# A two-layer decoder trunk: more buffers behind the attention transposes, bf16 weight copies in DRAM, and input norms computed inside the preceding MLP

## The reference

```python
def pool_mixer(a, w, scale):   # trailing mean over 2/4/8/16 positions, minus the token, then a linear map
def stick_breaking_attention(q, k, v):            # strictly causal, 8 heads of 64, no softmax
    z = einsum(q, k) / 8
    log_keep = where(mask, log_sigmoid(-z), 0)
    suffix = cumsum_from_the_right(log_keep) - log_keep
    weights = where(mask, exp(log_sigmoid(z) + suffix), 0)
    o = einsum(weights.astype(v.dtype), v)
for layer in range(2):
    xn = rmsnorm(h, mix_norm_g[layer])
    ...                                           # the two mixers of the layer, concatenated
    h = h + mixers @ w_out
    h = h + square(relu(rmsnorm(h, mlp_norm_g[layer]) @ w1)) @ w2
return rmsnorm(h, final_norm_g)
```

## Time and profile before

| | us |
|---|---|
| median of 3 runs | 3643.56 (3628.75 to 3654.9) |
| the profiled execution | 3627.29 |
| its span, slowest core (core 0) | 3625.8 (cores: 3571.9 to 3625.8) |
| PE busy | 2988.4 (82%) |
| DVE, ACT, POOL busy | 1440.2, 1375.5, 1126.3 |
| DMA packets | 381.62 MB, of which 189.02 MB on POOL's queue and 189.67 MB on SP's |

### The profile page before, as it was taken

One profiled execution on the slowest core, in us unless ns is written; L12 is line 12 of the kernel. 1 busy time (PEld: TensorE's weight loads), 2 busy tenths in 40 slices (PEclk: granted clock), 3 DMA queues, 4 the chain that ended last, 5 costly groups with the idle time before them and its releaser, 6 DMA issues.

```text
span 3625.8 us, 45548 instructions; the slowest of 8 cores (3571.9 to 3625.8 us)
## 1 busy us (share of the span) xinstructions
PE 2988.4 (82%) x14779; PEld 1287.9 (36%) x15073; DVE 1440.2 (40%) x1829; ACT 1375.5 (38%) x2277; POOL 1126.3 (31%) x1622
## 2 busy tenths in 40 slices
PE   1999867898888888788878688989889867888898
PEld 0444333343333333333333233333333323333343
DVE  2410426432434535763335363325444444434212
ACT  1244332525335353343434335242453435252522
POOL 1411125233123433633331342331244423432110
PEclk9999988999999999999989899999999988999999
DMA  7444684556677665656566555565666576567543
GB/s 180 67 68 79 125 171 72 74 91 96 121 172 97 112 90 97 137 88 88 88 103 132 133 86 73 90 101 107 128 96 99 91 169 85 93 96 153 104 76 82
DMA packets 466070, 381.62 MB, mean 105 GB/s; under 512 B 307760, under 2 KB 324400, under 8 KB 465840
## 3 DMA queue, kind: packets, MB, share of 16 engines
q0 software_dynamic: 103824, 189.02, 35.3%
q1 hardware_dynamic: 362016, 189.67, 24.1%
HBM read 454.30 MB, written 41.94 MB: 137 GB/s over the span
## 4 chain that ended last, share of the span: by engine, by line
PE 48%; DMA 24%; DVE 9%; POOL 6%; issue 5%; ACT 4%; SPq 4%; DVEq 0%; POOLq 0%; ACTq 0%
PE ps L543 44%; DMA Wk<-Wq 17%; DMA stg<-xT 5%; DVE P L1121 4%; POOL Wq L1135 4%; SPq L536 3%; PE ps L1160 2%; ACT ps L533 2%; PE ps L1105 1%; DMA oT<-stg 1%; DVE X_45 L619 1%; DMA mix<-dsp 1%; POOL Wq L1138 1%; DVE st_58 L936 0%; DVE h L650 0%
## 5 line engine op out<-in xcount | busy, mean ns | idle before, releaser
L543 PE MATMUL ps<-X_45,ring 128*128 128x512 bf16 x4746 | 1118.4, 389 | 23.0 <-DVE X_45 L619 6.1
L533 ACT ACTIVATE ps<-ps 128x512 f32<-128x512 f32 (+3 forms) x832 | 577.2, 698 | 836.7 <-PE ps L543 518.0
L569 POOL DMA_DIRECT2D ring<-wblk x720 | 391.4, 547 | 1391.3 <-PE ps L543 1180.6
L543 PE MATMUL ps<-mix,ring 128*128 128x512 bf16 x2980 | 756.0, 400 | 48.4 <-DMA mix<-dsp 28.9
L1135 POOL TENSOR_TENSOR Wq<-P 128x1022 bf16<-128x1022 f32 (+2 forms) x320 | 524.2, 1638 | 609.5 <-DVE P L1121 608.0
L1121 DVE TENSOR_TENSOR_SCAN P<-ps,carry,zeros 128x512 f32<-128x512 f32 x384 | 490.2, 1280 | 496.5 <-ACT ps L533 463.6
L543 PEld LDWEIGHTS ps<-X_45,ring 128*128 128x128 bf16 x4864 | 469.8, 100 | 592.4 <-issue 89.0
L650 DVE TENSOR_TENSOR h<-ps,h 128x512 f32<-128x512 f32 x384 | 263.7, 687 | 865.6 <-PE ps L543 845.1
L543 PE MATMUL ps<-ffB,ring 128*128 128x512 bf16 x2007 | 486.9, 384 | 2.3 <-issue 0.2
L543 PEld LDWEIGHTS ps<-mix,ring 128*128 128x128 bf16 x3072 | 297.2, 102 | 418.5 <-issue 126.2
L1160 PE MATMUL ps<-Wk,V 128*64 128x128 bf16 x2176 | 129.3, 236 | 337.2 <-DMA Wk<-Wq 336.1
(11 more groups left out here) (107 smaller groups left out, 1236.3 us busy)
## 6 DMA issues: line engine op xcount, KB each, us to landing
ring<-wblk POOLq DMA_DIRECT2D x720, 256.0 KB, 5.2
stg<-xT SPq DMA_DIRECT2D x128, 256.0 KB, 5.5
h<-xT SPq DMA_DIRECT2D x64, 256.0 KB, 16.2
hsp<-h SPq DMA_DIRECT2D x64, 256.0 KB, 5.1
h<-hsp SPq DMA_DIRECT2D x64, 256.0 KB, 8.0
oT<-stg SPq DMA_DIRECT2D x64, 256.0 KB, 3.3
Wk<-Wq SPq DMA_TRANSPOSE x320, 3.6
csp<-mix SPq DMA_DIRECT2D x8, 512.0 KB, 5.1
```

Of the source, the lines that this page charges most:

```text
L533: return Req("act", lambda e: e.activation(out=out, in_=in_, func=func, **kw), reads, writes, dur, bias=bias)
L543: ins = pe.matmul(out, lhsT=l, rhs=r, start=(first and i == 0), stop=(last and i == n - 1), skip_group_check=True)
L569: yield Req("pool", (lambda slot, b: lambda e: e.dma_start(out=self.ring[:, slot, :], in_=self.wblk[b]))(slot, b), [], [self.Lring[slot]], ...
```

## The change

Five things are changed.

1. `NWT` goes from 4 to 7 landing buffers, and the planned landing of a transpose from 3.1 to 7.0 us. Room in SBUF comes from `chain_pool`: two ping-pong buffers and a bf16 buffer become one (`PS`), the shifted adds run in place with all operands read from right to left, and the bf16 result overlays the same buffer.
2. A DRAM tensor `wbf` keeps a bf16 copy of every weight block. The first load of a block still casts from `wblk`; then SP stores the slot to `wbf` (`keep_block`), and the slot cannot be reused until that store has read it (`release`). Later loads of the block read `wbf`. First loads fall in F00 (88), M00 (20) and S00 (72).
3. `prefetch_x` for the next F stage is started right after the last input projection of the current one, so its norm matmuls, squares and scalings stand in that stage's output projection and MLP.
4. The first F stage has its own `start_x`: `x` is loaded straight into `h` (16 transfers, once), and squares and scalings read `h`.
5. In S, `load_mix` is started ahead of the reload of `h`.

```diff
-NWT = 4
+NWT = 7
...
     def ring_fiber(self):
         for n, b in enumerate(self.order):
             slot = yield self.slots
+            src = self.wbf if b in self.Lwbf else self.wblk
...
+            if b not in self.Lwbf:
+                self.Lwbf[b] = LT("wbf")
+                self.busy.add(slot)
+                self.M.spawn(self.keep_block(slot, b), 0.5)
             self.loaded[n] = slot
+
+    def keep_block(self, slot, b):
+        yield self.dma(self.wbf[b], self.ring[:, slot, :], [self.Lring[slot]], [self.Lwbf[b]], ("keep", slot))
+        self.busy.discard(slot)
+        if slot in self.gone:
+            self.gone.discard(slot)
+            self.slots.free(slot)
...
+    def start_x(self):
+        X, LX = self.X[0], self.LX[0]
+        for t in range(2):
+            ts = slice(t * TT, (t + 1) * TT)
+            for c in range(8):
+                yield self.load_h(self.xT, None, 0, 0, t, c)
+        for t in range(2):
...
+            for c in range(8):
+                yield self.act(X[:, c, ts], self.h[:, c, ts], AF.Square, [self.Lh[c][t]], [LX[c][t]], TT, False)
+            yield from self.norm(X, LX, t, None, 0, self.to_X(t, 0))
+            self.xready.add((0, 0, t))
...
                 yield Req("pool", (lambda src, d, b0: lambda e: e.tensor_tensor(
+                    out=S1[:, b0:528][:, ::-1], in0=src[:, b0:528][:, ::-1], in1=src[:, b0 - d:528 - d][:, ::-1],
+                    op=ALU.add))(src, d, b0), [Ls], [L1], 1.15)
...
-        self.xfree = True
+        if nx:
+            self.M.spawn(self.prefetch_x(*nx), 1.0)
         yield from self.out_proj("F", s, u)
...
-                  key=("wk", k), lat=3.1)
+                  key=("wk", k), lat=7.0)
...
+        self.M.spawn(self.load_mix(s, u), -0.2)
         self.M.spawn(self.load_h_fiber(self.hsp, self.Lhsp, s, u, self.hfree, "S"), 0.0)
-        self.M.spawn(self.load_mix(s, u), 0.0)
...
-        M.spawn(self.prefetch_x(0, 0), -0.5)
+        M.spawn(self.start_x(), -0.5)
```

More of the change, by code:

```diff
@@ L568, in ring_fiber, with release @@
             slot = yield self.slots
-            yield Req("pool", (lambda slot, b: lambda e: e.dma_start(out=self.ring[:, slot, :], in_=self.wblk[b]))(slot, b),
-                      [], [self.Lring[slot]], 0.53, key=("ring", slot), lat=4.0, bias=1.0)
-            self.loaded[n] = slot
+            src = self.wbf if b in self.Lwbf else self.wblk
+            yield Req("pool", (lambda slot, b, src: lambda e: e.dma_start(out=self.ring[:, slot, :], in_=src[b]))(slot, b, src),
+                      [self.Lwbf[b]] if b in self.Lwbf else [], [self.Lring[slot]], 0.53, key=("ring", slot),
+                      lat=4.0, bias=1.0)
+            if b not in self.Lwbf:
+                self.Lwbf[b] = LT("wbf")
+                self.busy.add(slot)
+                self.M.spawn(self.keep_block(slot, b), 0.5)
+            self.loaded[n] = slot
+    def keep_block(self, slot, b):
[4 more added lines that the diff above has]
+            self.slots.free(slot)
+    def release(self, slot):
+        if slot in self.busy:
+            self.gone.add(slot)
+        else:
+            self.slots.free(slot)
     def take(self, n):
@@ L738, in mlp @@
                         if t == 1:
-                            self.slots.free(sl[j])
+                            self.release(sl[j])
                 self.use_scratch("ff")
@@ L744, in mlp @@
                     yield from w1(sl[0], j, t)
-                self.slots.free(sl[0])
+                self.release(sl[0])
             n = 8 if q == 0 else 4
@@ L750, in mlp @@
                     yield from w2(sl, c, t, q)
-                self.slots.free(sl[0])
-                self.slots.free(sl[1])
+                self.release(sl[0])
+                self.release(sl[1])
             if q == 1:
@@ L758, in mlp @@
                         if t == 1:
-                            self.slots.free(sl[2 * c - 8])
-                            self.slots.free(sl[2 * c - 7])
+                            self.release(sl[2 * c - 8])
+                            self.release(sl[2 * c - 7])
             self.ffgen += 1
@@ L857, in chain_pool, with stage_F @@
         return evac
-    def stage_F(self, s, u):
+    def stage_F(self, s, u, nx):
         X, LX = self.X[0], self.LX[0]
@@ L863, in stage_F @@
         self.use_scratch("l0")
-        self.M.spawn(self.load_h_fiber(self.xT, None, s, u, self.hfree, "F"), 0.5)
+        if (s, u) != (0, 0):
+            self.M.spawn(self.load_h_fiber(self.xT, None, s, u, self.hfree, "F"), 0.5)
         for i in range(4):
@@ L922, in out_proj @@
                 if t == 1:
-                    self.slots.free(sl[c])
+                    self.release(sl[c])
     def chain_v(self, s, u, n, v):
@@ L1008, in stage_M @@
                 for x in sl[0:4]:
-                    self.slots.free(x)
+                    self.release(x)
             for g in range(4):
@@ L1017, in stage_M @@
                 if t == 1:
-                    self.slots.free(sl[4 + g])
+                    self.release(sl[4 + g])
         yield from self.need_attention(2 * s + u)
@@ L1237, in main @@
             if kind == "F":
-                yield from self.stage_F(s, u)
                 nx = [x for x in self.stages[n + 1:] if x[0] == "F"]
-                if nx:
-                    self.M.spawn(self.prefetch_x(nx[0][1], nx[0][2]), 1.0)
+                yield from self.stage_F(s, u, nx[0][1:] if nx else None)
             elif kind == "M":
@@ L1253, in build @@
         self.loaded = {}
+        self.Lwbf = {}
+        self.busy = set()
+        self.gone = set()
         self.blk = 0
```

50 lines of the change are left out of this document (23 added, 27 removed).

## The result

The changed kernel takes 3185.54 us (median of 4 runs, 3177.98 to 3210.77), the kernel before, run beside it, 3636.15 (median of 4, 3619.26 to 3654.9). The ratio is 0.8771, 95% interval 0.8714 to 0.8828: faster by 12.3 per cent. The forecast was 3225 us with a range of 3105 to 3355.

The account below looks back on a forecast made before the run. PE was taken to bound the kernel, losing time to late transposes (336.1 us) and half clock (486 us). 3627.3 - 258 - 80 - 33 - 40 - 14 + 10 + 8 = 3220, stated as 3225 us, range 3105 to 3355.

Parts of the forecast that it names:

- the likeliest case: The prediction's own forecast for the whole kernel, 3130 to 3330 us, given a chance of 0.60.
- waits for transposes: PE's value products waiting for late transposes: 336 us, less 58 beyond 3.7 us and 20 left in S00, -258 us.
- clock, as shorter busy time of PE: Whole core: granted clock rises from 0.933 towards F00's 0.97, worth at most 134 us; 0.6 of it taken, -80 us.
- start, waits up to the second tile's projection: First F stage: first projection at about 48 us, 19 us earlier, and second tile's waits gone; -33 us.
- input norms, waits outside the start: F stages: the 40.4 us of input waits "go", -40 us; 10 us charged for work moved into the stage before.
- `mix`: S stages: loading `mix` before the reload of `h` saves half of 28.9 us of waits, -14 us.
- The reason given for the copies: Weight loads: 540 non-casting loads save 0.9 us of engine time each, so the gain is in shorter transposes.
- 8 us longer for the stores: F00: stores of copies beside casting loads raise DMA share to 0.80, which fits; 8 us charged, ends 0 and 30.
- More: Rival: nearly all transposes land in 3 us, and waits and slow clock vanish; 3040 to 3130 us, chance 0.16.
- Half: Rival: PE arrives earlier but the chains do not; only 168 us of waits and 40 of clock go; 3350 us, 0.17.
- No change: Rival: another engine, nearest ACT in the MLP's first half, binds once PE stops waiting; 3600 to 3660 us, chance 0.04.
- Slower: Rival: POOL's reversed adds, each costing 5.1 us more than 1.04, eat the whole gain; chance 0.03.

Follow-up runs that it names:

- r_after: The changed kernel itself, word for word, timed and profiled a second time; median 3181.1 us, ratio 0.8749 to the kernel before.
- e_cast2: The changed kernel without bf16 copies: all 720 weight loads cast and nothing is stored; 3234.46 us, ratio 0.8888 to the kernel before.
- two-by-two: Four kernels: planned transpose landing 7.0 or 3.1 us (distance 64 or 48 matmuls), each with and without bf16 copies; ratios 0.8749, 0.8888, 0.9297, 0.9582.
- e_lat31_cast: The changed kernel with planned transpose landing back at 3.1 us and no bf16 copies; 3488.9 us, ratio 0.9582 to the kernel before.
- e_lat31: The changed kernel with planned transpose landing back at 3.1 us, copies kept; 3382.7 us, ratio 0.9297 to the kernel before.
- e_nwt4: The changed kernel with 4 landing buffers instead of 7; 3185.62 us, ratio 0.8744 to the kernel before.
- e_oldpre: The changed kernel with the next F stage's input loaded and normed after the F stage, beside the M stage, as before; 3238.69 us, ratio 0.893.
- e_nostart: The changed kernel with the first F stage's input loaded as before, by `prefetch_x`, and `h` loaded again; 3246.35 us, ratio 0.8963.
- b_lat7: The kernel before with only the planned transpose landing changed, 7.0 us instead of 3.1; 3350.7 us, ratio 0.9231.
- i_lat10_stg: The changed kernel with planned landings of 10.0 us for transposes, 5.0 for staged `x` loads, 6.5 for first weight loads; 3144.56 us, ratio 0.865.

## Why the prediction was right, and where its steps were off

The total was 40 us too high, inside the range, and the likeliest case was the one that came. How good its terms were depends on how they are counted, since the parts of the change cover for each other.

**By the rows of the two profiles.** PE's idle time fell from 3625.8 - 2988.4 = 637 to 3179.1 - 2917.2 = 262 us, its busy time by 71. Forecast and measured, by term:

| | forecast | rows of `before` and `r_after` |
|---|---|---|
| waits for transposes | -258 | -281 (336.1 to 54.9) |
| clock, as shorter busy time of PE | -80 | -71 |
| start, waits up to the second tile's projection | -33 | -38 |
| input norms, waits outside the start | -40 + 10 | -15 (40.4 to 25.0) |
| `mix` | -14 | -12 (28.9 to 17.3) |

The trace of the kernel before lacks 294 of PE's 15073 matmuls, so its busy time is rather larger than the row says, by an estimated 13 us (the 12.8 us in 68 idle moments that nothing released, of which `r_after` has none). Some 30 us of the 447 are in rows too small for this table. By this account the large terms, transposes and clock, were right in kind and in size; the terms err both ways, by 2 to 23 us, and that these errors partly cancel is luck. The waits came out at 54.9 us where 78 were forecast, with five over 4 us and S00 the worst of the stretches:

```profile
PE ps L1194 <- DMA Wk<-Wq: 22.4, 10, 6.4
```

(`r_after`, PE's waits in S00 alone: 22.4 of 54.9; in `e_cast2`, without stores, S00 has 8.8 of 80.0.) The clock came to 0.970, the cap of the prediction, and not to the 0.6 of the way there that it took. That the busy time fell by less than the 134 us of that cap fits the prediction's reason, that PE stands still in part of the slow time.

**By the kernels of the two-by-two.** `e_lat31_cast` has everything but distance and copies. These two are worth 0.9582 - 0.8749 = 0.083 of 3643, 303 us, where waits, clock and stores were forecast at -258 - 80 + 8 = -330; everything else is worth 152 us, where 77 were forecast. Part of this is the way of counting, as PE's line in `e_lat31_cast` shows:

```profile
PE 2965.9 (85%) x14781; PEld 1284.1 (37%) x15073; DVE 1443.4 (41%) x1829; ACT 1355.2 (39%) x2261; POOL 1128.2 (32%) x1622
```

Against the kernel before, 18 us of the waits for transposes (336.1 to 318.0) and 23 us of busy time are gone there already, and the prediction had these in its terms for waits and clock. From `e_lat31_cast` to `r_after` idle time falls by another 261 us and busy time by 49. So distance and copies bought mostly idle time, and only part of the clock's rise is theirs.

**The reason given for the copies.** The prediction had transposes landing between 3.0 and 3.6 us in the median; they land in 3.7. Copies do take 0.5 to 0.6 us from the median landing (3.7 to 3.1 us from `e_lat31_cast` to `e_lat31`, 4.2 to 3.7 from `e_cast2` to `r_after`), but the kernels with more distance have medians that are higher by 0.5 to 0.6. The traces show one thing that goes with it: more transposes are contended, 117 of 320 in `e_cast2` against 93 in `e_lat31_cast`, and 96 in `r_after` against 87 in `e_lat31`. Why was not tried. The prediction's main step, that the product moves 3.5 us away from a transpose that stays late, is what the table of the two-by-two shows (slack 0.4 to 3.7 us).

**Buffers.** The prediction took them together with the distance. `e_nwt4` shows that they do nothing.

**Everything else.** The terms of the kernels with one part undone:

- *Input norms*, forecast -30 net, measured -58 by `e_oldpre`, with an interval that takes in the -30. The step was wrong in one point: "They go" holds for the 25.2 us of waits for DVE, but the 15.2 for ACT became 25.0 inside the F stages (12.56 of them at once, shown under F00 below). That `e_oldpre` has 42 us more waits, near the 40 forecast, is luck: only 16 of them are for the input of F stages, and 25 are for the other norms, for which the kernel before waited no longer than the changed one. The charge of 10 was right in kind; F00 and F10 are 28 us longer than in `e_oldpre`. Why F11 (29 us) and S00 (22) are the stages that gain most was not tried.
- *Start*, forecast -33, measured -45 by `e_nostart`. The first projection was forecast for 48 us and came at 45.5; the second tile's waits were priced at 14 and gave 12. The remaining 7 us have no row of their own.
- *`mix`*, forecast -14: the row went from 28.9 to 17.3 us, -12; no kernel has it alone.
- 152 - 58 - 45 - 12 = 37 us are in no experiment. The 18 us of transposes and 23 of busy time above are about as much, but which part of the change brings them stays open. At the larger distance less is missing: `b_lat7` to `e_cast2` is 0.9231 - 0.8888, 125 us, against the same 115.

**F00.** Forecast 8 us longer for the stores; the stretch is 9.9 us longer (350.7 against 340.8), though 14.3 us of waits for the second tile are gone from it, which the forecast counted under the start. So the price in this stage is some 24 us, and the DMA share (0.75, against a forecast of 0.80) does not tell it. Stores without the moved input norms (`e_oldpre`) give 344 us by stage, moved norms without stores (`e_cast2`) 345, both 355, so each has its part. SP's queue in F00 from 130 us on (`r_after`) shows what the stores do there:

```profile
SPq L165 <- DMA ring<-wblk: 175.9, 60, 19.6
...
SPq L165 <- DMA stg<-xT: 18.4, 6, 5.8
```

A store of a copy waits on SP until its weight block has landed, 60 times and 175.9 us, and the loads of `x` for the next stage are queued behind it. PE then waits for a square of that input:

```profile
270.98 3.57 PE L543 MATMUL ps<-X,cbs 128*128 128x512 bf16 x8 [12.56 <-ACT X L533]
```

But this does not explain the price: the same wait is 9.89 us in `e_cast2`, which stores nothing, and in `i_lat10_stg`, where none of these waits is longer than 4.1 us, F00 takes 357 us. Where the rest goes stays open. The prediction named SP's list as a cost for the transposes, and priced stores by bytes alone. The Trainium skill (DMA: Bandwidth & Descriptors, Anatomy of one DMA) says that a semaphore wait happens on the issuing sequencer before dispatch; SP's row of 175.9 us agrees with it.

**The rivals.** *More* (3040 to 3130) is not reached, but the kernel with `lat=10.0` and corrected plans comes to within 15 us of it. *Half* (3350) is what `b_lat7` gives (3350.7), for another reason than the one named: there the waits go, and the other parts are missing. *No change* fell: ACT is busy 43 per cent, and of PE's waits for it only those for input squares grew clearly, by 10 us. *Slower* fell: POOL's reversed adds cost what the forward ones did, by this row of `r_after` (ns minimum, median, maximum):

```profile
L865 POOL TENSOR_TENSOR ps<-ps x48: 1037/1054/1532, 51.7 to 1848.9; 128x512 f32<-128x512 f32 x24, 128x524 f32<-128x524 f32 x8, 128x520 f32<-128x520 f32 x8, 128x516 f32<-128x516 f32 x8
```

## What to carry to other kernels

Where the order of the engines is fixed when the kernel is built, put into the plan the landing of a DMA as it is measured beside the traffic of the stage, not alone: here that one number was worth 7.7 per cent in the kernel before, and the buffers that came with it nothing. Before adding buffers, look whether the plan ever fills those it has. Look also at what stands behind a transfer on the list of the engine that issues it: here stores that wait for a weight load held SP's list for 439.6 us in 147 waits. And where several parts of a change cover for each other, compare a forecast term with the rows it was made from, and not only with the kernel that lacks the part.

## What the runs showed of the hardware that was not expected

- A transposing DMA (128x1024 bf16 or smaller, SBUF to SBUF) takes in the median about twice as long with two or more casting weight loads in flight at its middle (6.3 to 6.6 us, against 2.7 to 3.0 with none), and 5.3 to 5.5 us where three in four loads do not cast. The loads themselves fall from a median landing of 6.0 to 3.5 us, and from 1.78 to 0.94 us of the 16 engines.
- POOL's adds of 128x512 float32 with all operands read backwards and the result in place take 1.04 to 1.05 us in the median, as forward.
- Time at the lower clock falls with the waits, but is worth less than its length. Between `e_lat31_cast` and `r_after` PE's transpose waits fall by 263 us and the time at 1.2 GHz from 2 x 0.058 x 3489.1 = 405 to 191 us. A busy PE would have won half of these 214 us; its busy time fell by 49 (some 60, with the matmuls that the first trace lacks), since PE also stood still in slow time.
